# A two-layer hybrid block on one Trainium2 core: the second layer's projection with 12 whole tiles and 26 pairs in place of 16 and 24

## What is computed

```
h = rms_norm(x, g_pre)
u = einsum('bsd,dn->bsn', h, w_in)            # 1024 -> 8192
(pool_v, pool_g, conv_x, conv_gb, conv_gc, conv_g, sb_q, sb_k, sb_v, sb_g, merge) = split(u)
y_pool = pool_mixer(pool_v, pool_w, pool_scale) * silu(pool_g)
y_conv = conv_mixer(conv_x, conv_gb, conv_gc, conv_w, conv_b) * silu(conv_g)
y_sb   = stick_breaking_attention(sb_q, sb_k, sb_v) * silu(sb_g)      # 8 heads of 64
proj   = einsum('bsnw,nwd->bsnd', stack([y_pool, y_conv, y_sb]), w_branch)
out    = einsum('bsd,de->bse', sum(sigmoid(merge) * proj), w_out)
return x + rms_norm(out, g_post)
```

## Time and profile before

| | us |
|---|---|
| median of 3 runs | 2263.84 (2263.07 to 2267.44) |
| the profiled execution | 2266.77 |
| its span | 2265.0 |
| TensorE busy | 2218.3 |
| VectorE busy | 1487.2 |
| GpSimd busy | 1109.4 |
| ScalarE busy | 1030.3 |

### The profile page before, as it was taken

How to read it: one execution, slowest core, us unless ns; L and a number is a source line. 1 busy time by engine, 2 the same in 40 slices (tenths; PEclk the granted TensorE clock), 3 DMA queues, 4 the chain that set the end, 5 groups by cost and what they waited for, 6 DMA issues and landing times.

```text
span 2265.0 us, 30924 instructions
## 1 busy us (share of the span) xinstructions
PE 2218.3 (98%) x11281; PEld 1767.4 (78%) x11281; DVE 1487.2 (66%) x1963; ACT 1030.3 (45%) x1870; POOL 1109.4 (49%) x704
## 2 busy tenths in 40 slices
PE   9999989899999999999999999999999999999999
PEld 6778867676878888888887776777878888888886
DVE  7865858776497555589548885465685675545745
ACT  5564146675265555543546444342222332225653
POOL 2212135434147666656767320113557885556763
PEclk9999999999999999999999999999999999999999
DMA  4113364335225444765553400012222543348654
GB/s 162 38 38 100 118 183 111 101 111 192 90 78 186 168 154 153 269 193 173 161 162 89 136 29 29 29 47 74 99 75 64 176 170 112 112 143 280 190 167 149
DMA packets 153762, 289.41 MB, mean 128 GB/s; under 512 B 34915, under 2 KB 44387, under 8 KB 153612
## 3 DMA queue, kind: packets, MB, share of 16 engines
q1 hardware_dynamic: 153612, 287.44, 39.0%
HBM read 207.88 MB, written 79.51 MB: 127 GB/s over the span
## 4 chain that ended last, share of the span: by engine, by line
PE 87%; DVE 6%; ACT 2%; issue 2%; DMA 2%; POOL 1%; SPq 0%; DVEq 0%; POOLq 0%; ACTq 0%
PE bank L865 14%; PE bank L861 14%; PE bank L863 14%; PE bank L633 10%; PE bank L637 10%; PE bank L635 10%; PE bank L710 2%; PE bank L927 2%; PE bank L958 2%; PE bank L940 2%; ACT t L1000 1%; DVE t L1417 1%; PE bank L830 1%; PE bank L665 1%; PE bank L848 1%
## 5 line engine op out<-in xcount | busy, mean ns | idle before, releaser
L2071 POOL TENSOR_TENSOR t<-t,t 128x512 fp32r<-128x512 f32 (+1 forms) x539 | 859.4, 1606 | 955.4 <-ACT t L1000 929.2
L1000 ACT ACTIVATE t<-t 128x512 fp32r<-128x512 f32 (+2 forms) x734 | 468.8, 663 | 775.1 <-PE bank L865 344.9
L861 PE MATMUL bank<-t,t 128*128 128x512 f32 x1568 | 614.1, 392 | 6.1 <-DVE t L1795 4.6
L865 PE MATMUL bank<-t,t 128*128 128x512 f32 x1568 | 611.4, 390 | 1.0 <-DVE t L1417 0.9
L863 PE MATMUL bank<-t,t 128*128 128x512 f32 x1568 | 611.2, 390 | 0.9 <-POOL t L2071 0.9
L633 PE MATMUL bank<-t,t 128*128 128x512 f32 x1072 | 429.2, 400 | 0.8 <-ACT t L1000 0.8
L637 PE MATMUL bank<-t,t 128*128 128x512 f32 x1072 | 419.4, 391 | 2.4 <-DVE t L1417 1.9
L635 PE MATMUL bank<-t,t 128*128 128x512 f32 x1072 | 418.3, 390 | 1.5 <-POOL t L2071 1.5
L861 PEld LDWEIGHTS bank<-t,t 128*128 128x128 f32 x1568 | 295.0, 188 | 69.7 <-DVE t L1795 5.0
L863 PEld LDWEIGHTS bank<-t,t 128*128 128x128 f32 x1568 | 295.1, 188 | 64.0 <-POOL t L2071 1.8
L865 PEld LDWEIGHTS bank<-t,t 128*128 128x128 f32 x1568 | 295.0, 188 | 63.6 <-DVE t L1417 2.2
(11 more groups left out here) (248 smaller groups left out, 2463.0 us busy)
## 6 DMA issues: line engine op xcount, KB each, us to landing
t<-in_w SPq DMA_DIRECT2D x87, 512.0 KB, 3.6
hid_scr<-t SPq DMA_DIRECT2D x112, 256.0 KB, 2.1
t<-hid_scr SPq DMA_DIRECT2D x112, 256.0 KB, 2.7
t<-in_wf SPq DMA_DIRECT2D x80, 256.0 KB, 3.3
t<-in_wf SPq DMA_DIRECT2D x36, 512.0 KB, 4.3
g_scr<-t SPq DMA_DIRECT2D x36, 512.0 KB, 2.9
t<-g_scr SPq DMA_DIRECT2D x72, 256.0 KB, 3.6
t<-in_wo SPq DMA_DIRECT2D x24, 512.0 KB, 3.6
```

The source lines that it names most:

```text
L861: e.matmul(ps, hi, XH, start=start, stop=False)
L865: return e.matmul(ps, hi, XL, start=False, stop=stop)
L1000: return e.activation(out, in_, ACT.Copy, **kw)
L2071: return e.tensor_tensor(out, x, high.bitcast(F32), ALU.subtract)
```

## The change

The four tiles of the attention's gates (`sg`) become two pairs, the first two of now 26. With 12 whole tiles left, the whole tiles end before the last head pair's attention, and the first 14 products (`FILL`, two pairs) lie between the steps of that attention. Since banks 2 to 7 are then in use, these 14 take turns in banks 0 and 1, each after the product before the last has been read; later products use banks 2 to 7 as before. Two GpSimd steps of the convolution (`zx`, `yg`) get a later rank. The pooling's matmuls (`pm`, banks 0 and 1) wait for the two last of the 14 to be read.

```diff
-WHOLE, TWOS = 16, 24
+WHOLE, TWOS = 12, 26
+FILL = 14
+def two_bank(n):
+    return n % 2 if n < FILL else TWO_BANKS[(n - FILL) % 6]
...
-    o = [att[0][0], att[0][1], att[1][0], att[1][1], att[0][2], att[1][2]] + att[2] + att[3] + gates
-    rest = [("pg", 0), ("pg", 1), ("pv", 0), ("pv", 1), ("pg", 2), ("pg", 3), ("pv", 2), ("pv", 3)]
+    o = [att[0][0], att[0][1], att[1][0], att[1][1], att[0][2], att[1][2]] + att[2] + att[3] + gates[:0]
+    rest = gates + [("pg", 0), ("pg", 1), ("pv", 0), ("pv", 1), ("pg", 2), ("pg", 3), ("pv", 2), ("pv", 3)]
...
-        q.wait_ge(done("pc", g - 1, f) if g else done("evd", last))
+        q.wait_ge(*([done("pc", g - 1, f)] if g else [done(*x) for x in K.two_read(FILL - 2 + f)]))
...
     def two_bank_free(self, n):
-        if n >= 6:
+        if n < 2:
+            return self.bulk.evacuations(max(b for b in range(self.bulk.last["P4"] + 1) if self.bulk.jobs[b].bank == n))
+        if n < FILL:
+            return self.two_read(n - 2)
+        if n >= FILL + 6:
             return self.two_read(n - 6)
...
-        add("pool", "zx", i, rank=0.5)
+        add("pool", "zx", i, rank=4.5)
...
-        add("pool", "yg", i, rank=0.5)
+        add("pool", "yg", i, rank=4.5)
```

More of the change, by code:

```diff
@@ L910, in pm @@
     def pm(g, f):
-        last = [b for b in range(B.last["P4"] + 1) if B.jobs[b].bank == f][-1]
-        q.wait_ge(done("pc", g - 1, f) if g else done("evd", last))
+        q.wait_ge(*([done("pc", g - 1, f)] if g else [done(*x) for x in K.two_read(FILL - 2 + f)]))
         q.wait_ge(done("pf", g), done("plw"))
@@ L965, in gp @@
         hi, lo = M.weight(v)
-        ps = banks[TWO_BANKS[(7 * i + n) % 6]]
+        ps = banks[two_bank(7 * i + n)]
         for k in range(4):
@@ L1338, in qe @@
         q.wait_ge(done("gp", i, 0), *[done(*x) for x in K.stage_freed(a)])
-        copy(M.stage[a % 3][:, 0:512], banks[TWO_BANKS[7 * i % 6]][:, :]).then_inc(*tick("qe", i))
+        copy(M.stage[a % 3][:, 0:512], banks[two_bank(7 * i)][:, :]).then_inc(*tick("qe", i))
     def bs(h, x):
@@ L2020, in qd @@
         q.wait_ge(done("gp", i, n), *[done(*y) for y in after])
-        tt(out, old, banks[TWO_BANKS[(7 * i + n) % 6]][:, :], ALU.add).then_inc(*tick("qd", i, x))
+        tt(out, old, banks[two_bank(7 * i + n)][:, :], ALU.add).then_inc(*tick("qd", i, x))
     def bm1d(h, x):
@@ L2554, in end_bank_free @@
             return [("pc", 3, bank)]
-        return self.two_read(max(n for n in range(7 * TWOS) if TWO_BANKS[n % 6] == bank))
+        return self.two_read(max(n for n in range(7 * TWOS) if two_bank(n) == bank))
     def two_read(self, n):
@@ L2562, in two_bank_free @@
     def two_bank_free(self, n):
-        if n >= 6:
+        if n < 2:
[3 more added lines that the diff above has]
+        if n >= FILL + 6:
             return self.two_read(n - 6)
-        return [("ss", a, 3, p) for a in range(2) for p in (10, 11)] if n < 4 else [("stc", 3, 7, g) for g in range(4)] + [("vc", 3, 1)] if n == 4 else [("so", 3, 7)]
+        return [("ss", a, 3, p) for a in range(2) for p in (10, 11)] if n < FILL + 4 else [("stc", 3, 7, g) for g in range(4)] + [("vc", 3, 1)] if n == FILL + 4 else [("so", 3, 7)]
     def two_place(self, c, k):
```

## The result

The changed kernel takes **2267.75 us** (median of 20 runs, 2265.32 to 2272.69) against 2264.00 (20 runs, 2262.64 to 2267.44) before: 1.0017 times as long, 95% interval 1.001 to 1.0023. That is 3.75 us slower; 2.2 were forecast, and the time lies within the range. The profiled execution took 2268.49 us with a span of 2266.4, 1.7 us more than that of before.

What follows compares the result with a forecast made beforehand. TensorE, busy for 98% of the span, was taken to bound the kernel. Waits of 4.5 + 3.2 + 2.0 less 7.3 saved gave +2.4 us, of which 0.2 was dropped: 2266.0 us, range 2260.5 to 2270.5.

Steps and rivals of the forecast that it cites:

- Removed: On TensorE, 24 products go, 5.4 us less, and the first pair product's wait goes, 1.9 us less.
- The late chain: After the last whole tile, VectorE sums, weight parts and a load delay the second scan; TensorE waits 4.5 us.
- T: The end of the last whole tile on TensorE, from which the prediction counts its times.
- one meeting of each kind: VectorE adds meeting GpSimd: one with a low part, about 1.1 us, one with the differences, 2.1 us.
- The collisions: VectorE's adds slowed by GpSimd operations ahead of the first scans: 3.2 us taken, from nothing to 4.3 us.
- the third sums with three evictions: VectorE before T: 12 adds taken as 8 us with evictions, against 10.8 us of products; they just fit.
- The second block: Third and fourth score steps wait for the second block's scans: 2.0 us, from 1.2 to 2.5.
- rival 3: The clock falls once in the waits, 3.3 us at half speed, giving away 1.7 us: 2267.7 us; chance 0.16.
- the 7 to 11 named as the sign: TensorE idle for 7 to 11 us in some 20 us right after the last whole tile.
- The wait at the pooling: TensorE's wait before the pooling's matmuls stays: busy for only 0.12 us of the 3.2 from 1680 us.
- rival 2: Two banks too few: products under the long scans wait for VectorE's reads, 4 us slower, 2270.0 us; chance 0.12.
- rival 1: VectorE in time at the last head pair's scans, only about 2 us of waits: 2258.5 us; chance 0.10.

Runs made afterwards that it cites:

- the run with the wait filled: Changed kernel with TensorE repeating the first matmul of the first pair product 11 times ahead of it: 2269.11 us, 1.0015 times the kernel before.
- the second timing: The changed kernel as it is, timed once more beside the kernel before: 2268.11 us, 1.0015 times the kernel before.
- the two with the next sum late: Changed kernel with the second pair's first sum of weights behind the last head pair's first four scans, run twice: 2272.67 us (1.0031) and 2271.87 us (1.0027).
- the one with both sums late: Changed kernel with the third sums and the next pair's sum of weights behind the first four scans: 2263.01 us, 0.9987 times the kernel before.
- no product below: Changed kernel with no product of a pair under the last head pair, all starting after it: 2277.18 us, 1.0056 times the kernel before.
- the half step: Half of the change, 14 whole tiles and 25 pairs, 7 products under the last head pair: 2262.36 us, 0.9987 times the kernel before.
- the last version: 14 whole tiles and 25 pairs, with VectorE's first convolution block behind the last pooling block and the eighth pair's sums of weights: 2259.17 us, 0.997.

## Why the prediction was right

**Removed.** The 24 products are gone, and so is the first pair product's wait, at the place named. Nothing to correct.

**The late chain** was sized by its steps. Sums done: T + 10.4 forecast with one meeting of each kind, T + 10.9 measured. Load there: T + 17.2 against 17.0. Transposes: T + 18.3 against 18.4. The collisions were 2.2 us (three low parts) and 1.6 (one add), 3.8 against the 3.2 taken. Two sums of the prediction are off, and nothing hangs on them: TensorE's steps add up to 10.5 us, not 10.6, and the third sums with three evictions to 9.6 (12 x 0.65 + 3 x 0.6), not 8; VectorE was idle for 0.46 us before the last eviction, so they did fit. The Trainium skill, "SBUF — State Buffer", section "SBUF: two separate sides", has GpSimd and a VectorE operation with two SBUF inputs lock the same ports against each other for whole instructions; the add of 2.26 us beside the 2.35 us of the differences agrees.

**The second block.** 2.0 us were taken (1.2 to 2.5). The two profiles of the change show 1.43 and 0.24, but the fourth score step comes at 1505.17 in both: in the second TensorE, longer at half clock, only arrives 1.2 us later. The size of the term is 1.43, 0.6 less than taken.

**The step that failed is the clock.** "The waits that I expect are broken by products, and I add nothing": the clock did fall, after the first of them, for 6.8 us, which is rival 3 and longer than the 3.3 us it was priced at. For this reason too the idle time is 5.5 us and not the 7 to 11 named as the sign: a part of it is filled by slow matmuls. The number survived because the price was not paid: the run with the wait filled shows that TensorE at half clock was no later than VectorE's low parts and the load. The prediction's reason for its nothing was another, so that is luck, and narrow: with 10.2 us at half clock 0.24 us of waiting were left at the fourth score step. By the Trainium skill, "TensorE: Matmul & The Clock Gate", "Part 1: The HAM clock gate", an idle array falls back to half clock; here it did after 2.56 us, and in the kernel before it did not after the 3.2 us of the earlier trace rows.

**The rest.** The wait at the pooling was taken to stay; it is 2.08 us long in place of 3.08, a microsecond that I did not foresee. The block's last two operations on VectorE began in a gap between two of GpSimd's and took 1.4 us, not 3.5 as before; a sum of weights ahead of them took 1.8 instead of 0.7. Whether the later rank of the convolution's GpSimd steps has to do with it was not tested. Two banks (rival 2) show no sign: TensorE is never idle from 1506.5 to 1553.8 us. VectorE in time (rival 1) did not come by itself, and its price came only in part when the third sums were moved: in the profile the stretch from the first score step of the second layer's attention to the last product is 4.9 us shorter than before (1280.55 to 2021.84 against 1281.51 to 2027.67), near the 5.3 forecast, but the medians differ by 2.5 us.

**The sum.** From the first score step of the second layer's attention (1281.51 us before, 1281.56 after) to the start of the projection's last product (2027.67, 2028.43) it is 0.7 us longer in both profiles of the change. By parts: -5.4 -1.9 -1.0 (pooling) +5.5 (idle time in the five waits) +0.8 (0.16 us of drain at each, as the prediction counts it) +2.8 (half of the 5.6 us that TensorE was busy in the 6.8 at half clock; at full clock it would have waited as long) = +0.8. So the waits came to 9.1 us for 9.7 forecast. The medians differ by 3.75 us, in the second timing by 2.0. The prediction took the rows of one profiled execution for a median run; that execution lies 2.8 us above its median and that of the change 0.7, and where these 2 us sit was not seen. So the profiles bear out the mechanism, and that the median came within 1.75 us of the forecast is in part luck. "No change that can be told" was too much: the interval, 1.001 to 1.0023, leaves 1 out.

## What to carry to other kernels

When work is taken off the engine that sets the time, look at what its cover hid: here the four whole tiles of the gates gave VectorE time for sums; taking two of them away gained 3.2 us, taking all four lost 3.75. The longest wait in a profile is where a late chain is first met, not what makes it late; moving the step it names (GpSimd's differences) moved the wait, moving the work ahead of the chain (VectorE's sums, and with them the order of TensorE) removed it. A wait on a copy or a matmul is followed back to the engine that holds the buffer before anything is moved.

## What the runs showed of the hardware

A wait of the same length at one place brought the clock down or not. Before the last pooling matmuls TensorE waited 2.06 to 2.09 us in eight profiles; in the two with the next sum late and the one with both sums late the granted clock then fell to 0.50 for 3.4 us, in the other five (the change twice, the third sums late, the differences first, no product below) it did not. After 3.08 us there it fell in the run with the wait filled and not in the kernel before. What decides it is not shown.

A small operation of VectorE can cost as much as a large one: in the half step a product of 128 x 16 elements took 1.25 us while GpSimd worked, in the last version 0.17, where no GpSimd operation ran beside it.
